# A two-block transformer kernel: the last expert-up product drained bank by bank, context prepared beside it, latent norm spread over its tiles

## The reference

```python
x = x + einsum('tk,tkd->td', w, v_sel)            # end of block one: expert up product
x_in = x     * (1 + scale)   + shift              # block two, layer 0
c_in = h_ctx * (1 + scale_c) + shift_c
p  = x_in @ w_in;  pc = c_in @ w_in               # _even_mixer
q  = _rms(q_latent, q_norm) @ w_qb                # latents: 512 (q) + 512 (kv) + 64 (rope)
kv = _rms(kv_latent, kv_norm) @ w_kvb
conv = cb * _short_conv(cc * cu, conv_w)
_rms(x, g) = x * rsqrt(mean(x * x) + EPS) * g
```

## Time and profile before

| | |
|---|---|
| median of 3 runs | 4376.3 us (4373.22 to 4386.44) |
| profiled execution | 4375.69 us, its span 4373.9 us |
| busy | PE 93%, DVE 56%, POOL 41%, ACT 38% of the span |
| mean granted TensorE clock | 0.951 |

### The profile page before, as it was taken

The page is one execution under the profiler, slowest core; times in us unless marked ns, Lnnn a source line. Parts: engine busy times, 40 slices in busy tenths (PEclk is TensorE's granted clock), DMA queues, the critical chain, the costliest instruction groups (busy, mean ns, idle before and its releaser), DMA issues.

```text
span 4373.9 us, 69728 instructions
## 1 busy us (share of the span) xinstructions
PE 4065.3 (93%) x27828; PEld 3599.7 (82%) x27828; DVE 2452.0 (56%) x3083; ACT 1653.3 (38%) x2322; POOL 1802.5 (41%) x984
## 2 busy tenths in 40 slices
PE   7999998899899799999999999799999898979998
PEld 6666667889899799999999999777888656858887
DVE  5787776543699558777333577623221233657646
ACT  3122235544355467333344333312222223233574
POOL 5666662234488455444444444321222101222223
PEclk9999999999999885999999999899999989989999
DMA  5667664345455343555555455522222202213323
GB/s 188 245 261 280 253 259 158 116 164 185 163 183 191 144 142 96 183 188 185 211 220 209 175 183 184 190 77 77 96 96 87 76 29 77 97 64 128 126 88 135
DMA packets 132420, 679.28 MB, mean 155 GB/s; under 512 B 43680, under 2 KB 49952, under 8 KB 52512
## 3 DMA queue, kind: packets, MB, share of 16 engines
q1 hardware_dynamic: 89952, 641.77, 40.0%
q10 hardware_dynamic: 42304, 35.21, 2.4%
HBM read 664.35 MB, written 12.58 MB: 155 GB/s over the span
## 4 chain that ended last, share of the span: by engine, by line
PE 76%; DVE 15%; ACT 3%; issue 2%; DMA 2%; POOL 1%; DVEq 0%; ACTq 0%; SPq 0%; POOLq 0%
PE banks L387 45%; PE banks L2068 17%; DMA ring<-in_stream_dram 2%; PE banks L2169 1%; PE banks L1905 1%; DVE w_lo L368 1%; PE banks L1981 1%; ACT w_hi L360 1%; DVE eq L1422 1%; PE banks L1886 1%; PE banks L2225 1%; PE banks L2051 1%; DVE eq L1421 1%; PE banks L1860 1%; PE banks L2118 1%
## 5 line engine op out<-in xcount | busy, mean ns | idle before, releaser
L368 POOL TENSOR_TENSOR w_lo<-ring,w_hi 128x1024 fp32r<-128x1024 f32 x552 | 1406.3, 2552 | 2410.4 <-ACT w_hi L360 2408.9
L387 PE MATMUL banks<-h_hi,w_hi 128*128 128x256 f32 (+1 forms) x5392 | 1665.7, 309 | 172.0 <-DVE w_lo L368 68.1
L387 PE MATMUL banks<-h_hi,w_lo 128*128 128x256 f32 (+1 forms) x5392 | 1645.8, 305 | 0.0
L387 PE MATMUL banks<-h_lo,w_hi 128*128 128x256 f32 (+1 forms) x5392 | 1644.9, 305 | 0.0
L360 ACT CAST w_hi<-ring 128x1024 fp32r<-128x1024 f32 x1024 | 1021.8, 1047 | 1150.4 <-PE banks L387 485.9
L387 PEld LDWEIGHTS banks<-h_hi,w_hi 128*128 128x128 f32 x5392 | 1035.0, 192 | 246.6 <-issue 129.6
L368 DVE TENSOR_TENSOR w_lo<-ring,w_hi 128x1024 fp32r<-128x1024 f32 x472 | 647.1, 1371 | 883.0 <-ACT w_hi L360 880.4
L387 PEld LDWEIGHTS banks<-h_hi,w_lo 128*128 128x128 f32 x5392 | 1034.1, 192 | 51.6 <-issue 0.7
L387 PEld LDWEIGHTS banks<-h_lo,w_hi 128*128 128x128 f32 x5392 | 1033.2, 192 | 51.2
L2068 PE MATMUL banks<-wp_hi,w_hi 128*128 128x256 f32 x2048 | 577.8, 282 | 7.4 <-DVE wp_lo L1493 7.4
L2068 PE MATMUL banks<-wp_hi,w_lo 128*128 128x256 f32 x2048 | 577.4, 282 | 0.0
(11 more groups left out here) (370 smaller groups left out, 4557.4 us busy)
## 6 DMA issues: line engine op xcount, KB each, us to landing
ring<-in_stream_dram SPq DMA_DIRECT2D x608, 1024.0 KB, 4.8
g_out<-stage ACTq DMA_DIRECT2D x32, 256.0 KB, 2.6
g_in<-g_out ACTq DMA_DIRECT2D x8, 1024.0 KB, 6.4
X<-in_x_in_dram SPq DMA_DIRECT2D x2, 1024.0 KB, 7.0
b_st<-in_ssm_b_dram ACTq DMA_DIRECT2D x8, 256.0 KB, 8.0
c_st<-in_ssm_c_dram ACTq DMA_DIRECT2D x8, 256.0 KB, 8.5
X<-in_x_in_dram ACTq DMA_DIRECT2D x1, 2048.0 KB, 7.6
x_save<-X ACTq DMA_DIRECT2D x1, 2048.0 KB, 7.2
```

Of the source, the lines that this page charges most:

```text
L368: eng.tensor_tensor(w_lo[:, t.par, s], ring[:, t.slot, s], w_hi[:, t.par, s].bitcast(F32), ALU.subtract).then_inc(lo_done[h], 1)
L387: m = pe.matmul(bank(b, n), w[:, t.par, k], x(k), start=(k == 0 and w is w_hi and x is xh), stop=(k == BLK - 1 and x is xl))
```

## The change

1. In `up_pe` the last four tiles stand outside the loop; in the very last, PE signals each bank as it is finished (`up_summed`). DVE's `spill` takes banks one by one, in `up0` as in `up1`.
2. The context is loaded early in `up1` (after 8 tiles), modulated in place and cast by ACT in four groups between weight casts (after 28, 36, 44 and 52 tiles), and its `h2_lo` is made by POOL in four subtractions of 128x1024 between weight splits (after 48, 52, 56 and 60).
3. The tokens' part is prepared bank by bank: `lat_in` and `lat_hi` on ACT, `lat_lo` on DVE; PE waits in the first `lat` tile before every second block. ACT casts `lat` tile 1 after the sixth bank. `x_save` is written after the last bank; DVE's first `lat` copy waits for it.
4. Squares, sums, roots and scaling of the latents lie between the `lat` tiles; the last sum is in the ninth tile, and the rope swap in the first `conv` tile. `cvu` is cleared in the first `lat` tile, and the two additions to `mods` stand before `up0`.
5. The semaphore `x_moved` takes the place of `x_saved` and `xx_loaded`, and `back` that of `ctx_loaded` and `sk_loaded`; counts of `hm_hi`, `h2_pool` and `h2_ready` later in the program move accordingly.

ACT:

```diff
@@ -735,31 +735,62 @@
...
-            up_act(1)
...
-            act.wait_ge(S("spilled"), 16)
-            act.dma_start(x_save, X[:]).then_inc(S("x_saved"), 16)
-            act.dma_start(xc[:], ctx_in).then_inc(S("ctx_loaded"), 16)
...
-                for q in range(4):
-                    act.wait_ge(S("hm_ready"), q + 1 + 4 * n)
-                    act.copy(h2_hi[:, 4 * q:4 * q + 4], hm[:, 4 * q:4 * q + 4]).then_inc(S("hm_hi"), 1)
...
-            for j in range(9):
-                hi_split(act, Tile("lat", j).next())
...
+            up_act(1, 0, 2)
+            act.wait_ge(mm_done, G0["up1"])
+            act.dma_start(xc[:], ctx_in).then_inc(S("back"), 16)
+            up_act(1, 2, 7)
+            act.wait_ge(S("back"), 96)
+            act.wait_ge(S("spilled"), 8)
+            act.wait_ge(mm_done, G0["up1"] + 16)
+            for q in range(4):
+                for k in range(4 * q, 4 * q + 4):
+                    m = act.activation(xc[:, k], xc[:, k], ACT.Identity, bias=md(0, 0, k, 1), scale=md(0, 1, k, 1))
+                m.then_inc(S("hm_ready"), 1)
+                act.wait_ge(S("hm_ready"), q + 1)
+                act.copy(h2_hi[:, 4 * q:4 * q + 4, T:], xc[:, 4 * q:4 * q + 4]).then_inc(S("hm_hi"), 1)
+                up_act(1, (7, 9, 11, 13)[q], (9, 11, 13, 16)[q])
...
+            def lat_in(b):
+                act.wait_ge(S("spilled"), 8 + b + 1)
+                for k in (2 * b, 2 * b + 1):
+                    m = act.activation(hm[:, k], X[:, k], ACT.Identity, bias=md(0, 0, k, 0), scale=md(0, 1, k, 0))
+                m.then_inc(S("hm_ready"), 1)
+            def lat_hi(b):
+                act.wait_ge(S("hm_ready"), 4 + b + 1)
+                act.copy(h2_hi[:, 2 * b:2 * b + 2, 0:T], hm[:, 2 * b:2 * b + 2]).then_inc(S("hm_hi"), 1)
+            act.wait_ge(S("wp_ready"), 128)
+            lat_in(0)
+            for b in range(8):
+                if b < 7:
+                    lat_in(b + 1)
+                lat_hi(b)
+                if b == 5:
+                    hi_split(act, Tile("lat", 0).next())
+            act.dma_start(x_save, X[:]).then_inc(S("x_moved"), 16)
...
+            def lat_root(f):
...
+            for j in range(1, 9):
+                hi_split(act, Tile("lat", j).next())
+                lat_square(j - 1)
+                if j == 5:
+                    lat_root(0)
+            lat_root(1)
```

POOL:

```diff
@@ -1034,10 +1065,18 @@
...
                     gates_high(n, i, 2)
-            for ph_ in ("up0", "down1", "up1"):
-                with pool.Fori(0, 16, 1) as i:
+            for ph_, a, b in (("up0", 0, 16), ("down1", 0, 16), ("up1", 0, 12), ("up1", 12, 13), ("up1", 13, 14),
+                              ("up1", 14, 15), ("up1", 15, 16)):
+                if ph_ == "up1" and a:
+                    q = a - 12
+                    pool.wait_ge(S("hm_hi"), q + 1)
+                    pool.wait_ge(mm_done, G0["up1"] + 48)
+                    pool.tensor_tensor(h2_lo[:, 4 * q:4 * q + 4, T:], xc[:, 4 * q:4 * q + 4],
+                                       h2_hi[:, 4 * q:4 * q + 4, T:].bitcast(F32), ALU.subtract)\
+                        .then_inc(S("h2_pool"), 1)
+                with pool.Fori(0, b - a, 1) as i:
                     for j in range(4):
-                        lo_split(pool, Tile(ph_, j, i, 4).next(), 0)
+                        lo_split(pool, Tile(ph_, j, i, 4, skip=4 * a).next(), 0)
```

DVE:

```diff
@@ -1493,14 +1532,22 @@
...
-                dve.wait_ge(mm_done, G0[f"up{half}"] + 64)
-                for b in range(8):
-                    x = X[:, 2 * b:2 * b + 2]
-                    dve.tensor_tensor(x, x, bank(b).rearrange("p (a t) -> p a t", a=2), ALU.add)\
-                        .then_inc(S("spilled"), 1)
...
+            def spill(half, b):
+                if b < 7:
+                    dve.wait_ge(S("up_summed"), 7 * half + b + 1)
+                else:
+                    dve.wait_ge(mm_done, G0[f"up{half}"] + 64)
+                x = X[:, 2 * b:2 * b + 2]
+                dve.tensor_tensor(x, x, bank(b).rearrange("p (a t) -> p a t", a=2), ALU.add)\
+                    .then_inc(S("spilled"), 1)
+            for layer in range(2):
+                L(dve.tensor_scalar(mods[:, layer, 16:32], mods[:, layer, 16:32], 1.0, None, ALU.add))
             up_dve(0)
+            for b in range(8):
+                spill(0, b)
             for k in range(16):
                 for j in range(4):
                     t = Tile("down1", 4 * k + j)
...
-                        for s_ in range(2):
-                            m = dve.tensor_scalar(hm[:, k, s_ * T:(s_ + 1) * T], xs(k, s_), md(n, 1, k, s_),
-                                                  md(n, 0, k, s_), ALU.mult, ALU.add)
-                    m.then_inc(S("hm_ready"), 1)
-                for q in range(4):
-                    s_ = slice(4 * q, 4 * q + 4)
-                    dve.wait_ge(S("hm_hi"), q + 1 + 4 * n)
-                    dve.tensor_tensor(h2_lo[:, s_], hm[:, s_], h2_hi[:, s_].bitcast(F32), ALU.subtract)\
-                        .then_inc(S("h2_ready"), 1)
-            mixer_in(0, lambda k, s_: (X, xc)[s_][:, k])
-            dve.wait_ge(S("x_saved"), 16)
...
+            def lat_lo(b):
+                dve.wait_ge(S("hm_hi"), 4 + b + 1)
+                s_ = slice(2 * b, 2 * b + 2)
+                dve.tensor_tensor(h2_lo[:, s_, 0:T], hm[:, s_], h2_hi[:, s_, 0:T].bitcast(F32), ALU.subtract)\
+                    .then_inc(S("h2_ready"), 1)
+            for b in range(8):
+                spill(1, b)
+                if b >= 2:
+                    lat_lo(b - 2)
+            lat_lo(6)
+            lat_lo(7)
+            def lat_norm(f):
...
+            for j in range(9):
+                t = Tile("lat", j)
+                lo_split(dve, t.next(), 1)
+                if j == 0:
+                    L(dve.memset(cvu[:], 0.0))
+                    dve.wait_ge(S("x_moved"), 16)
+                if j == 8:
+                    lat_norm(1)
+                dve.wait_ge(mm_done, t.done())
+                dve.tensor_copy(lat[:, j] if j < 8 else rk[:], bank(t.bank())).then_inc(acc_free[t.bank()], 1)
+                dve.wait_ge(acc_free[t.bank()], t.a0 // 4 + 2)
+                dve.sem_inc(S("lat_read"), 1)
+                if j == 5:
+                    lat_norm(0)
```

PE:

```diff
@@ -2059,22 +2109,27 @@
...
+                def tile(j, i, skip):
+                    first, last = skip == 0, skip == 60
...
+                        if last and j == 3 and k % 2 and k < BLK - 1:
+                            m.then_inc(S("up_summed"), 1)
...
-                with pe.Fori(0, 15, 1) as i:
+                    tile(j, None, 0)
+                with pe.Fori(0, 14, 1) as i:
                     for j in range(4):
-                        tile(j, i, False)
+                        tile(j, i, 4)
+                for j in range(4):
+                    tile(j, None, 60)
...
-            pe.wait_ge(S("spilled"), 16)
...
-            for j in range(9):
-                dense(pe, Tile("lat", j), xh2, xl2, N2)
-            pe.wait_ge(S("lat_read"), 9)
-            pe.matmul(bank(5), C("perm_m"), rk[:], start=True, stop=True).then_inc(S("swap_done"), 1)
-            for k in range(8):
...
+            def lat_wait(b):
+                return lambda: pe.wait_ge(S("h2_ready"), b + 1)
...
-            with pe.Fori(0, 8, 1) as i:
...
+            def rope_swap():
+                pe.wait_ge(S("lat_read"), 9)
+                pe.matmul(bank(5), C("perm_m"), rk[:], start=True, stop=True).then_inc(S("swap_done"), 1)
+            pe.wait_ge(S("h2_pool"), 4)
+            for j in range(9):
+                t = Tile("lat", j)
+                if j < 4:
+                    pe.wait_ge(S("spilled"), 8 + t.bank() + 1)
+                dense(pe, t, xh2, xl2, N2,
+                      before={2 * b: lat_wait(b) for b in range(8)} if j == 0 else {4: lambda: lat_sum(7)} if j == 8 else {})
+                if 0 < j < 8:
+                    lat_sum(j - 1)
+            for j in range(4):
+                dense(pe, Tile("conv", j), xh2, xl2, N2, before={} if j else {3: rope_swap})
+            with pe.Fori(0, 7, 1) as i:
...
-                    dense(pe, Tile("conv", j, i, 4), xh2, xl2, N2)
+                    dense(pe, Tile("conv", j, i, 4, skip=4), xh2, xl2, N2)
```

More of the change, by code:

```diff
@@ L655, in down_act, with up_act @@
                 act.activation(ab[:, row], bank(t.bank(), T), ACT.Gelu).then_inc(acc_free[t.bank()], 1)
-            def up_act(half):
-                with act.Fori(0, 16, 1) as i:
+            def up_act(half, a=0, b=16):
+                with act.Fori(0, b - a, 1) as i:
                     for j in range(4):
-                        hi_split(act, Tile(f"up{half}", j, i, 4).next())
+                        hi_split(act, Tile(f"up{half}", j, i, 4, skip=4 * a).next())
             with act.Fori(0, SELECT, 1) as i:
@@ L758, in _ @@
                 act.activation(lsq[:, k % 2], lat[:, k], ACT.Square).then_inc(S("lsq_ready"), 1)
-            for f in range(2):
```

(12 more changed lines are left out.)

59 lines of the change are left out of this document (16 added, 43 removed).

## The result

The changed kernel takes 4348.2 us (median of 20 runs, 4328.9 to 4369.2). The kernel before, run beside it and counted with the three runs shown ahead, takes 4387.5 us (median of 20 runs, 4363.6 to 4402.7). The ratio is 0.9916, with a 95% interval of 0.9900 to 0.9931: the change is faster by 0.84%, or 37 us (the two medians lie 39.3 us apart). Forecast were 40.0 us less, from a base of 4375.7 us. The saving is met within its interval; the time of 4336 us is missed by 12, nearly all of which is the base.

A forecast was written before the change was run, and what follows sets the result against it. PE, busy 93% of the span, was taken as the bound, so only its waits and slow clock counted. Gains 4.4 + 42.4 less 6.8 made 40.0 us, from 4375.7 to 4335.7 (forecast 4336), range 4324 to 4349.

The forecast's parts named there:

- Term 2: End of `up1` to second `conv` tile: bank-by-bank drain and hidden norm gain 42.4 us, bounds 35 to 46.9.
- rival (c): Before the second `conv` tile: the norm is not hidden and the 7.4 us hole stays; 4343 us, chance 0.04.
- Term 3: Context work in `up1`: POOL's subtractions hold up DVE's operations and PE waits; loss 6.8 us, bounds 0 to 11.
- rival (a): In `up1`, POOL never gets in front of `wp_lo`, so 6.0 us come back; 4330 us, chance 0.28.
- rival (b): More slow PE clock: three `up1` holes at 1.4 us each, plus 1.5 for `lat` 0 hand-offs; 4342 us, chance 0.13.
- Rival (e): Slower than before: holes do not heal and each of the last 16 `up1` tiles pays; 4391 us, chance 0.03.
- (d): The context load in `up1` holds up the weights, at most 11.8 us shown once; 4347 us, chance 0.06.
- Term 1: End of `up0`: early spills close PE's 2.85 us hole and save 1.6 of slow clock; gain 4.4 us.
- the small ones: Moved `mods` additions, `cvu` cleared under a `lat` tile, four unrolled tiles: taken as 0, 1 us either way.

The follow-up runs named there:

- e3_norm_at_end: Changed kernel, but the latents' squares, sums, roots, scaling and swap stand behind the ninth `lat` tile again; `lat` and `conv` took 478.6 us, 11.5 more.
- e9_after_again: The changed kernel unchanged, run a second time: median 4349.4 us of 6 runs, ratio 0.9910 to the kernel before.
- e5_ctx_after_wplo: Changed kernel, but POOL's 128x1024 context subtraction also waits until DVE has written `wp_lo` of the tile; `up1` took 370.9 us.

## Why the prediction was right, and where it failed

**Term 2, the drain and the norm (gain 42.4): right.** Measured 43.2 in the first pair of executions, and 43.7 on the mean of seven. The path from `up1`'s last matmul to the second `conv` tile is 2962.4 - 2836.9 = 125.5 us, where the sum gave 124.7. Its parts stand in the trace: a wait of 0.84 us before `lat` for 0.8; the hand-offs every 1.50 us; a hole of 2.49 us before the seventh pair of blocks for 3; the sums; no wait before the second `conv` tile, so rival (c) is out, and `e3_norm_at_end` prices it at 11.5 us. The clock falls behind the 2.49 us as it did behind the 7.40, but not always. Three rows of the changed kernel, after `up0`, after the third hole in `up1` and after the hole in `lat` 0, and one of `e9_after_again` after its hole in `lat` 0 (the clock stands behind the matmuls):

```profile
2098.00:2101.00 3.00, 3.00 (x28) 1.00 0.63 265
2788.00:2791.00 3.00, 2.92 (x14) 0.53 0.77 317
2849.00:2853.00 4.00, 3.70 (x9) 0.58 0.93 393
```

```profile
2842.50:2846.50 4.00, 3.95 (x17) 1.00 0.93 393
```

Of the eight executions with this hole of 2.49 us, six show 0.57 to 0.68 over the 4 us behind it, and two 1.00 (`e9_after_again`, `e5_ctx_after_wplo`). The stage takes 467.0 to 467.2 us with the lower clock (without `e3`, which has the norm at the end) and 465.6 without it: the 1.4 of the sum for this clock measured 1.5, but isn't paid every time.

**Term 3, the context in `up1` (loss 6.8): right.** Four waits of 0.9 to 1.9 us, 6.1 in all, and `up1` 375.7 on the mean of six executions against 369.1: 6.6. POOL did get in front of `wp_lo` at each of the three groups that follow a split, and the first group cost 0.91 us in the other way, for 0.8 in the sum; rival (a), with this term at 0, is out. In the changed kernel's first execution the clock fell behind one of the four holes (0.53 after the one at 2788; 1.00 behind the others), which is part of rival (b), but on the mean of the six executions the stage lost only 0.5 us more than the waits. One reading in this term is too narrow: `wp_hi` multiplies one tile, `ab`, by a constant, and still ended with POOL, so "when both read two operands from SBUF" doesn't cover the row it was drawn from. Rival (e) is out: the holes healed in one tile. The context and saved tokens land in time, so (d) is out too; the DMA issues, which answer to the earlier trace rows:

```profile
xc<-in_ctx_in_dram ACTq DMA_DIRECT2D x1, 2048.0 KB, 10.2
```

```profile
x_save<-X ACTq DMA_DIRECT2D x1, 2048.0 KB, 6.3
```

**Term 1, the end of `up0` (gain 4.4): its mechanism right, its worth not.** The wait is gone and the clock there is 1.00 (first window above). But the step "2.85 + 1.6 = 4.4" takes for granted that what follows runs as before, and it doesn't: `down1` begins at 5.65 us a tile in ten of ten. Over fourteen executions the term measures 0.2 us, give or take some 5. That `down1` came out at -4.8 in the first pair, next to the forecast, is luck. The rows of before could have warned: the earlier trace rows and the `up` tiles' 5.65 / 48 = 0.118 us stood in the prediction, and the spacing behind the hole in `down1`, 0.113, was not read.

With stage means the sum is 0.2 + 43.7 - 6.6 = 37.3, and 41.1 with the 3.8 us behind `conv` that the forecast had at 0, against 40.0 forecast and 36.9 by the ratio (4387.5 x 0.0084; 30 to 44 by its interval). That the total was met may be luck in part: term 1 and the stages behind `conv` miss by about 4 us each, in opposite directions.

**The base and the untouched code: the step that failed.** "The profiled execution took 4375.7 us, so 4335.7; it lies 0.6 below the median shown, which changes nothing." It changed nothing against three runs. Against twenty it lies 11.8 us low: this kernel's executions spread over 39 us, and the three shown were 4373 to 4386. The 40.0 us saved from a base of 4387.5 would be 4347.5, beside a measured 4348.2. The range, 4324 to 4349, was built from the terms' bounds and 1 us either way for the small ones; what untouched code does from one execution to the next (`up0` starting anywhere in 31 us, `down1` anywhere in 15) was put at nothing. The prediction had the number, "0.3%, 13 us", and used it for its chances but not for its range. So the measured median lies 0.8 us below the range's upper end and the profiled execution 0.3 above it, for a saving that was right within its interval.

## What to carry to other kernels

- Price a change by the stages it touches, cut at the same instruction in both traces, and keep the spread of the untouched ones apart: here three terms came out within 1 us each in one pair of traces (one of them by luck) while the spans disagreed with their sum by 14. A base of three runs with a spread of 0.3% needs at least that much on each side of the range.
- Before you add an operation on GpSimd beside a chain of short DVE operations, look at what would wait for the shared reads: cut it small and put it where the chain is not. Here waiting behind a GpSimd operation of 2.41 us cost an operation of 0.43 us another 2.0.
- A hole closed ahead of a long, regular stage is worth only what the stage keeps: read its matmul spacing in both traces, and in more than one execution of each.

## What the runs showed of the hardware that was not expected

- Identical matmul streams ran at two spacings, 5.44 and 5.65 us for 48 (276 against 281 ns each as the trace gives them), PE never idle, at a granted clock of 1.00 both times. The stage held one spacing for as little as 3 tiles and as long as the whole stage of 64.
- The same hole of 2.49 us was followed by a granted clock of 0.57 to 0.68 over 4 us in six executions, and of 1.00 in two.
- One kernel's stage of sparse matmuls took 263.7 us once and 248.1 once; the difference was the granted clock, 0.52 and 1.00 over 30 us at the same place of the program.
- A wait 1400 us into the kernel was 13.7, 25.4, 31.9 or 38.3 us in the executions read, in code that was the same; neighbouring values lie 11.7, 6.5 and 6.4 us apart.
